# Post-norm and two stage-norm statistics taken token by partition on 128x4, and the first two units of the last up stage in one pass

## The chip, the cores and the metric

One core of a Trainium2 chip runs the whole program. The metric is device time in microseconds (us) of one execution; the median of three runs of the kernel before is 2634.64 us (2630.85 to 2634.64). TensorE's clock has two levels here, 2.4 GHz (granted clock 1.00 in the profile) and 1.2 GHz (0.50).

## What is computed

Two transformer blocks on 512 tokens of width 1024, in fp32. The change touches only the RMS norms:

```python
def rmsnorm(x, g):
    y = xf * lax.rsqrt(jnp.mean(xf * xf, axis=-1, keepdims=True) + RMS_EPS)
    return (y * g).astype(x.dtype)

# second block
f = swiglu(rmsnorm(x, ffn1_pre_g), ffn1_w_gate, ffn1_w_up, ffn1_w_down)
x = x + 0.5 * rmsnorm(f, ffn1_post_g)
y = hybrid_mixer(rmsnorm(x, mix_pre_g), ...)
x = x + rmsnorm(y, mix_post_g)
f = swiglu(rmsnorm(x, ffn2_pre_g), ffn2_w_gate, ffn2_w_up, ffn2_w_down)
x = x + 0.5 * rmsnorm(f, ffn2_post_g)
```

## The kernel before

Activations lie with the feature on the partition and the 512 tokens in the free dimension, as eight tiles of 128x512 (k = 0 to 7). Weights come in units of 128x1024 fp32 (eight 128x128 blocks, one output tile). Each unit is split: ScalarE makes w_hi (`high_part`, line 1075), GpSimd makes w_lo in two halves (line 336), and TensorE does 24 matmuls of 128x512 for it: per k one with h_hi and one with h_lo against w_hi (`mm_hi`), and then eight of h_hi against w_lo (`mm_lo`). These are fp32r. Units alternate between two weight buffers and between PSUM banks 0 and 1; SP loads the next raw weights when GpSimd has used the last. All matmuls go through one helper and are put down to line 363.

The norm is applied late: a unit is computed with the raw x times the gain, and the result is multiplied by 1/rms (`rst`) when VectorE takes it from PSUM (`take`, line 1525). A sum of squares over the features is a sum over partitions, so TensorE makes it, in plain fp32 (each such matmul is two records in the trace). The statistics are numbered by r. This change touches five of them:

- r = 3, 5, 7, the post norms after `down2`, `out2` and `down3`. VectorE sums the squares of the eight tiles into `acc` (line 2065), `stat_of_acc` (line 408) multiplies `acc` by a 128x128 block of ones, so that every partition of bank 2 holds the sums of all 512 tokens; ScalarE takes the square root from bank 2 to bank 3 (`stat_root`, line 1085), and VectorE the reciprocal in bank 3 (`rms_rstd`, line 1541). `post_scale` (line 2075) multiplies each tile by bank 3. Then per tile GpSimd adds it to x (line 348), ScalarE rounds h_hi and squares x (`residual_hi`, lines 1089 and 1093), and VectorE makes h_lo (`low_x`, line 1547). After r = 7 there is only the final addition and the store.
- r = 4 and 6, the norms ahead of the `mix` stage and of `up3`, the third up stage. They are made inside `first_unit`: as each tile k comes, TensorE does the two `mm_hi` of the stage's first unit, and one 128x512 matmul of the squares with ones into bank 2. After k = 7 it signals the sum, does the unit's eight `mm_lo`, and goes on to the second unit. VectorE's reciprocal goes to `rst` in SBUF and `ffn_dve` or the mix loop begins with `take`.

In `up3` ScalarE's order is: the root of r = 6, then (in `ffn_act`) a Silu of the first unit's taken result, and only then `high_part` of the stage's third unit.

Of the kernel before, what the change touches and what calls it, by code (L numbers as in the profile page):

```python
# [24 lines left out]
ACT = mybir.ActivationFunctionType  # L25
# [5 lines left out]
D = 1024  # L31
# [63 lines left out]
def build_program(nc, io):  # L95
# [3 lines left out]
    def sb(name, shape, dt=F32, scope=ctx):  # L99
        return scope.enter_context(nc.sbuf_tensor(name, shape, dt))  # L100
# [3 lines left out]
    def sem(name):  # L104
        if name not in sems:
            sems[name] = ctx.enter_context(nc.semaphore(name))
        return sems[name]

    with ctx:
# [12 lines left out]
        sel = sb("sel", [128, 8])  # L122
        rst = sb("rst", [128, T])
        eps, lnx_eps = sel[:, 3:4], sel[:, 4:5]
        psum = ctx.enter_context(nc.psum_tensor("psum", [128, 8, 512], F32))
# [143 lines left out]
        def tok(n):  # L269
            return slice(128 * n, 128 * n + 128)  # L270
# [90 lines left out]
        def _(pe):  # L361
# [48 lines left out]
            def first_unit(g, o, r, nset):  # L410
# [9 lines left out]
                for k in range(KD):  # L420
                    if k % 4 == 0:
                        open_low(g, k // 4)
                    last = mm_lo(psum[:, o.slot], g.slot, k, h_hi[:, k], k == KD - 1)
                last.then_inc(sem("unit_used"), 1)

            def spread_heads(bank, stat, c):
# [466 lines left out]
            def ffn_mm(f, hset, up, down, o, stat=None):  # L893
                if stat is None:
                    first_unit(Index(FIRST[up]), Index(o), 6, hset)
                else:
                    unit(Index(FIRST[up]), Index(o), h_hi, h_lo, ("h_ready", 8 * hset))
                    stat_of_acc(stat)
                unit(Index(FIRST[up] + 1), Index(o + 1), h_hi, h_lo)
                with pe.Fori(0, KF - 1) as i:  # L900
# [11 lines left out]
            ffn_mm(1, 3, "up2", "down2", 109, 1)  # L912
            stat_of_acc(2)
            first_unit(Index(FIRST["mix"]), Index(161), 4, 4)


# [143 lines left out]
            with pe.Fori(0, 4) as i:  # L1060
                for c in range(2):
                    unit(Index(FIRST["out2"] + c, i, 2), Index(254 + c, i, 2), y2_hi, y2_lo, ("y_ready", 8))
            stat_of_acc(3)
            ffn_mm(2, 6, "up3", "down3", 262)
            stat_of_acc(4)


        @block.scalar
        def _(act):
# [12 lines left out]
            def stat_root(r):  # L1082

                act.wait_ge(sem("stat_sum"), r + 1)
                act.activation(p3, p2, ACT.Sqrt, bias=eps, scale=1.0 / D).then_inc(sem("stat_root"), 1)

            def round_x(gains, k):
# [305 lines left out]
            down_tiles("down2", lambda last, i, c: square_f(109 + 2 * KF, last, i, c))  # L1393
            stat_root(3)

# [13 lines left out]
            residual_hi(0, "mix_pre")  # L1409
            stat_root(4)  # L1410
            with act.Fori(0, 2) as i:
# [96 lines left out]
            with act.Fori(0, 4) as i:  # L1508
                for c in range(2):
                    high_part(Index(FIRST["out2"] + 2 + c, i, 2))  # L1510
                    square_f(254, Index(FIRST["out2"] + c, i, 2), i, c)
            stat_root(5)
            residual_hi(1, "ffn2_pre")
            stat_root(6)
            ffn_act(2, "up3", 262)
            down_tiles("down3", lambda last, i, c: square_f(262 + 2 * KF, last, i, c), 1)
            stat_root(7)


        @block.vector  # L1520
        def _(dve):
# [15 lines left out]

            def rms_rstd(r, dst=rst[:]):

                dve.wait_ge(sem("stat_root"), r + 1)  # L1540
                dve.reciprocal(dst, p3).then_inc(sem("stat_rstd"), 1)  # L1541
                dve.wait_ge(sem("stat_rstd"), r + 1)

            def low_x(nset, gains, k):
# [510 lines left out]
            def f_tiles(stage, o, r, a, gains, factor, per_unit):  # L2055

                dve.memset(acc[:], 0.0).then_inc(sem("acc_done"), 1)
                with dve.Fori(0, 4) as i:
                    for c in range(2):
# [7 lines left out]
                                          ALU.mult, ALU.mult).then_inc(sem(f"freed{ob.slot}"), 1)  # L2067
                rms_rstd(r, p3)
                for c in range(2):
# [18 lines left out]
            residual_low(0, 4, "mix_pre")  # L2088
            rms_rstd(4)

# [161 lines left out]
            residual_low(1, 6, "ffn2_pre")  # L2252
            rms_rstd(6)
            ffn_dve(2, "up3", 262)
# [158 lines left out]
```

## Time and profile before

| | |
|---|---|
| median of three runs | 2634.64 us |
| profiled execution, its own time | 2633.49 us |
| its span, first to last instruction | 2631.4 us |
| mean granted TensorE clock | 0.966 |
| busy: PE, PEld (weight loads), DVE, ACT, POOL | 94%, 76%, 38%, 36%, 40% |
| chain that ended last | PE 87%, DVE 6%, ACT 4%, issue 2% |

The profile is read as follows. A row of the timeline or of the chain begins with its start in the span and its duration, in us; in the timeline rows of one kind in a row are merged, with their count. The end of a matmul is modelled, so the spacing of starts is what tells its price. A row of a stretch (window) holds per engine the busy us and the number of instructions, and then the granted clock (PEclk), the share of the DMA engines and GB/s.

### The profile page before, as it was taken

Reading aid. Unit: us, or ns where it says so; the run is one execution under the profiler, and the core shown is the slowest. Engines: PE = TensorE matmul, PEld = TensorE weight load, DVE = VectorE, ACT = ScalarE, POOL = GpSimd, SP = SyncE. Lnnn points to the kernel's source line nnn. Section 1 sums busy time; section 2 is a strip of 40 time slices with the busy share of each in tenths; the row PEclk is TensorE's granted clock in tenths of the full one; section 3 lists DMA queues with packets and bytes.
Section 4 is the critical chain, followed back from the end, with each engine's and each line's share of the span. In section 5 each row is a group of like instructions: output and inputs, shape, how many; then the busy total and the mean of one; then the engine's idle time right before and its main releaser. Section 6 shows DMA issues by size and latency. Waiting matters only on the chain.

```text
span 2631.4 us, 39196 instructions
## 1 busy us (share of the span) xinstructions
PE 2478.2 (94%) x14008; PEld 1986.8 (76%) x14008; DVE 991.8 (38%) x1684; ACT 954.8 (36%) x1283; POOL 1051.7 (40%) x756
## 2 busy tenths in 40 slices
PE   8989898889999999999998999998999998999997
PEld 6866777767788888788886677767777776788885
DVE  3244484554555522322214343334222244422213
ACT  3233342223566632444323122213443442444321
POOL 3211131014455555555555442342333344555554
PEclk9889999999999999999999999998999999999998
DMA  4111110013232233322332221121222222223332
GB/s 169 50 40 33 49 56 27 3 33 112 80 96 96 96 108 98 96 96 96 99 101 100 72 70 60 56 80 41 72 72 79 64 85 91 64 96 96 97 102 88
DMA packets 56744, 205.24 MB, mean 78 GB/s; under 512 B 6828, under 2 KB 7596, under 8 KB 56268
## 3 DMA queue, kind: packets, MB, share of 16 engines
q1 hardware_dynamic: 55152, 196.45, 23.0%
q10 hardware_dynamic: 1504, 7.49, 0.8%
q8 instruction: 71, 1.16, 0.2%
q14 instruction: 17, 0.14, 0.0%
HBM read 201.81 MB, written 2.10 MB: 77 GB/s over the span
## 4 chain that ended last, share of the span: by engine, by line
PE 87%; DVE 6%; ACT 4%; issue 2%; POOL 0%; DMA 0%; DVEq 0%; ACTq 0%; SPq 0%
PE psum L363 85%; DVE ml_qk L2181 1%; PE psum L541 1%; DVE tmp L1669 1%; ACT tmp L1166 1%; ACT w_hi L1075 0%; POOL x L348 0%; PE psum L975 0%; DVE psum L1541 0%; DVE zm L1739 0%; DVE inv L1840 0%; DVE rst L1541 0%; DVE psum L1530 0%; DVE tmp L2075 0%; ACT ml_qk L1454 0%
## 5 line engine op out<-in xcount | busy, mean ns | idle before, releaser
L336 POOL TENSOR_TENSOR w_lo<-raw,w_hi 128x512 fp32r<-128x512 f32 x732 | 1021.2, 1416 | 1549.2 <-ACT w_hi L1075 1549.2
L363 PE MATMUL psum<-h_hi,w_hi 128*128 128x512 f32 x2192 | 900.6, 411 | 57.5 <-DVE h_lo L1547 26.5
L363 PE MATMUL psum<-h_lo,w_hi 128*128 128x512 f32 x2192 | 871.7, 398 | 0.0
L1075 ACT ACTIVATE w_hi<-raw 128x1024 fp32r<-128x1024 f32 x366 | 386.0, 1055 | 834.4 <-PE psum L363 815.6
L363 PEld LDWEIGHTS psum<-h_hi,w_hi 128*128 128x128 f32 x2192 | 423.6, 193 | 191.8 <-issue 86.9
L363 PE MATMUL psum<-h_hi,w_lo 128*128 128x512 f32 x2192 | 550.6, 390 | 0.0
L363 PEld LDWEIGHTS psum<-h_lo,w_hi 128*128 128x128 f32 x2192 | 423.4, 193 | 90.7 <-issue 6.9
L363 PEld LDWEIGHTS psum<-h_hi,w_lo 128*128 128x128 f32 x2192 | 412.1, 188 | 87.5 <-issue 1.4
L1525 DVE TENSOR_TENSOR tmp<-psum,rst 128x512 f32<-128x512 f32 x108 | 74.7, 692 | 369.9 <-PE psum L363 369.5
L363 PE MATMUL psum<-hid_hi,w_hi 128*128 128x512 f32 x528 | 208.7, 395 | 0.0
L363 PE MATMUL psum<-hid_lo,w_hi 128*128 128x512 f32 x528 | 208.4, 395 | 0.0
L363 PE MATMUL psum<-hid_hi,w_lo 128*128 128x512 f32 x528 | 134.9, 395 | 0.0
L2065 DVE TENSOR_TENSOR acc<-acc,sq 128x512 f32<-128x512 f32 x24 | 30.8, 1283 | 242.9 <-ACT sq L1338 242.9
L363 PEld LDWEIGHTS psum<-hid_lo,w_hi 128*128 128x128 f32 x528 | 99.1, 188 | 24.1
L363 PEld LDWEIGHTS psum<-hid_hi,w_lo 128*128 128x128 f32 x528 | 99.1, 188 | 24.1
L363 PEld LDWEIGHTS psum<-hid_hi,w_hi 128*128 128x128 f32 x528 | 99.1, 188 | 24.1 <-DVE tmp L2038 0.2
L2049 DVE TENSOR_TENSOR hid_lo<-tmp,hid_hi 128x512 f32 x66 | 52.7, 798 | 60.7 <-ACT hid_hi L1387 60.7
L1383 ACT ACTIVATE tmp<-tmp 128x512 f32<-128x512 f32 x44 | 27.8, 632 | 115.4 <-DVE tmp L1525 115.4
L1387 ACT ACTIVATE hid_hi<-tmp 128x512 f32 x66 | 41.7, 632 | 70.5 <-DVE tmp L2047 70.5
L1166 ACT ACTIVATE tmp<-tmp,soft_nb,q_scale 128x128 f32<-128x128 f32 (+3 forms) x64 | 36.7, 643 | 83.8 <-DVE soft_nb L1677 83.8
L1530 DVE TENSOR_TENSOR psum<-psum,rst 128x512 f32<-128x512 f32 x60 | 41.6, 694 | 56.5 <-PE psum L363 56.3
L2034 DVE SCALAR_TENSOR_TENSOR tmp<-psum,par,tmp 128x511 f32<-128x511 f32 x44 | 33.0, 750 | 71.1 <-ACT tmp L1375 71.1
(383 smaller groups left out, 2552.1 us busy)
## 6 DMA issues: line engine op xcount, KB each, us to landing
raw<-in_w SPq DMA_DIRECT2D x366, 512.0 KB, 3.6
x<-in_x SPq DMA_DIRECT2D x4, 512.0 KB, 6.1
tmp<-in_cmp_w ACTq DMA_DIRECT2D x1, 2048.0 KB, 7.5
x<-in_x ACTq DMA_DIRECT2D x1, 2048.0 KB, 7.8
out_y<-x SPq DMA_DIRECT2D x8, 256.0 KB, 2.1
mask<-in_mask ACTq DMA_DIRECT2D x1, 1536.0 KB
masks<-in_masks ACTq DMA_DIRECT2D x1, 768.0 KB, 9.3
lora<-in_lora ACTq DMA_DIRECT2D x1, 512.0 KB, 4.2
```

The costliest lines, as they stand in the source:

```text
L336: pool.tensor_tensor(w_lo[:, g.slot, part], raw[:, g.slot, part], w_hi[:, g.slot, part].bitcast(F32), ALU.subtract).then_inc(sem("lo_ready ...
L363: return pe.matmul(out, lhsT, rhs, start=start, stop=stop)
L541: last = pe.transpose(psum[:, 6 + r, tok(m)], att_s[t % 2][2 * g + r][:, tok(m)], ident[:])
L1075: act.activation(w_hi[:, g.slot], raw[:, g.slot], ACT.Copy).then_inc(sem("hi_ready"), 1)
L1166: last = act.activation(p, p, ACT.Exp, bias=soft_nb[:, t % 2, g, r:r + 1], scale=q_scale[:, at:at + 1])
L1383: act.activation(tmp[:, 2], tmp[:, 4], ACT.Silu).then_inc(sem("silu_done"), 1)
L1387: act.activation(tile_of(hid_hi, i), tmp[:, 3], ACT.Copy).then_inc(sem("hid_rounded"), 1)
L1525: dve.tensor_tensor(dst, psum[:, o.slot], rst[:], ALU.mult).then_inc(sem(f"freed{o.slot}"), 1)
L1530: dve.tensor_tensor(psum[:, o.slot], psum[:, o.slot], rst[:], ALU.mult)\
L2034: dve.scalar_tensor_tensor(tmp[:, c, 1:], psum[:, ob.slot, 0:T - 1], col("ffn_conv", 2 * KF + c + 2 * i), tmp[:, c, 1:], ALU.mult, ALU.add ...
L2049: dve.tensor_tensor(tile_of(hid_lo, i), tmp[:, 3], tile_of(hid_hi, i).bitcast(F32), ALU.subtract)\
L2065: dve.tensor_tensor(acc[:], acc[:], sq[:, ob.slot], ALU.add).then_inc(sem("acc_done"), 1)
```

## The change

`stat_of_acc` gives way to `post_stat` at r = 3, 5 and 7, and `first_unit` to `first_units` at r = 4 (one unit) and r = 6 (two units). The matrix and the moving operand change places: for each of four blocks of 128 tokens, the squares are the stationary 128x128 operand and one column of ones is moved, so that the sum of a token stands on the token's partition, 128x4 in all. Root and reciprocal then work on 128x4 (`stat4`). `spread_rstd` brings the four columns back to all partitions: a column broadcast to 128x128 as the stationary operand, times the identity (128 columns), four times, into bank 3; TensorE waits for the reciprocal ahead of it, and VectorE waits for `stat_spread` behind it. For r = 4 and 6 VectorE copies bank 3 to `rst` and waits for the copy (`keep_rstd`). In `first_units` with two units, per k the order on TensorE is the first unit's `mm_hi`, the four statistic matmuls, the second unit's `mm_hi`; then the first unit's `mm_lo`, `spread_rstd`, the second unit's `mm_lo`.

```diff
+            def spread_rstd(r):
+                pe.wait_ge(sem("stat_rstd"), r + 1)
+                for b in range(TB):
+                    last = mm(p3[:, tok(b)], stat4[:, 1, b:b + 1].to_broadcast([128, 128]), ident[:])
+                last.then_inc(sem("stat_spread"), 1)
+            def post_stat(a, r):
+                pe.wait_ge(sem("acc_done"), 9 * a + 9)
+                for b in range(TB):
+                    last = mm(p2[:, b:b + 1], acc[:, tok(b)], sel[:, 2:3])
+                last.then_inc(sem("stat_sum"), 1)
+                spread_rstd(r)
+            def first_units(g, o, r, nset, count):
+                for n in range(count):
+                    open_unit(g + n)
+                    open_bank(o + n)
+                for k in range(KD):
+                    pe.wait_ge(sem("h_ready"), 8 * nset + k + 1)
+                    mm_hi(psum[:, o.slot], g.slot, k, h_hi[:, k], h_lo[:, k], k == 0)
+                    pe.wait_ge(sem("squared"), KD * r + k + 1)
+                    for b in range(TB):
+                        last = pe.matmul(p2[:, b:b + 1], tmp[:, k, tok(b)], sel[:, 2:3], start=k == 0 and b == 0,
+                                         stop=k == KD - 1, skip_group_check=True)
+                    if k == KD - 1:
+                        last.then_inc(sem("stat_sum"), 1)
+                    if count == 2:
+                        mm_hi(psum[:, (o + 1).slot], (g + 1).slot, k, h_hi[:, k], h_lo[:, k], k == 0)
+                for n in range(count):
+                    for k in range(KD):
+                        if k % 4 == 0:
+                            open_low(g + n, k // 4)
+                        last = mm_lo(psum[:, (o + n).slot], (g + n).slot, k, h_hi[:, k], k == KD - 1)
+                    last.then_inc(sem("unit_used"), 1)
+                    if n == 0:
+                        spread_rstd(r)
...
-                    first_unit(Index(FIRST[up]), Index(o), 6, hset)
+                    first_units(Index(FIRST[up]), Index(o), 6, hset, 2)
...
-            stat_of_acc(2)
-            first_unit(Index(FIRST["mix"]), Index(161), 4, 4)
+            post_stat(2, 3)
+            first_units(Index(FIRST["mix"]), Index(161), 4, 4, 1)
...
-            stat_of_acc(3)
+            post_stat(3, 5)
             ffn_mm(2, 6, "up3", "down3", 262)
-            stat_of_acc(4)
+            post_stat(4, 7)
...
+            def stat_root4(r):
+                act.wait_ge(sem("stat_sum"), r + 1)
+                act.activation(stat4[:, 0], p2[:, 0:TB], ACT.Sqrt, bias=eps, scale=1.0 / D).then_inc(sem("stat_root"), 1)
...
+            def rms_rstd4(r):
+                dve.wait_ge(sem("stat_root"), r + 1)
+                dve.reciprocal(stat4[:, 1], stat4[:, 0]).then_inc(sem("stat_rstd"), 1)
+                dve.wait_ge(sem("stat_spread"), r - 2)
+            def keep_rstd(n):
+                dve.tensor_copy(rst[:], p3).then_inc(sem("stat_kept"), 1)
+                dve.wait_ge(sem("stat_kept"), n)
```

The calls of `stat_root` and `rms_rstd` for r = 3 to 7 become `stat_root4` and `rms_rstd4`, with `keep_rstd` after r = 4 and 6. The statistics r = 0, 1 and 2 stay as they are.

## Rows read from the trace of the kernel before

**Rows 1.** Page, chain that ended last: share of the span by engine.

```profile
PE 87%; DVE 6%; ACT 4%; issue 2%; POOL 0%; DMA 0%; DVEq 0%; ACTq 0%; SPq 0%
```

**Rows 2.** Chain that ended last, 2225 to 2262 us: start, duration, what.

```profile
2230.41 1.14 PE psum L363 x2
...
2232.27 3.38 DVE psum L1541
...
2235.67 0.70 DVE tmp L2075
...
2239.63 22.54 PE psum L363 x72
```

**Rows 3.** Chain that ended last, 2608 to 2632 us.

```profile
2613.55 1.14 PE psum L363 x2
```

**Rows 4.** Small operations, each by its line: duration min/median/max in ns.

```profile
L1283 ACT ACTIVATE rs<-psum,sel x4: 260/264/268, 557.6 to 569.7; 128x8 f32<-128x8 f32 x4
...
L2210 DVE RECIPROCAL ml_small<-ml_small x4: 177/178/178, 1875.5 to 2096.8; 128x4 f32<-128x4 f32 x4
```

**Rows 5.** Timeline of TensorE, matmuls with few moving columns, and what follows.

```profile
65.61 12.46 PE L363 MATMUL psum<-blocks,tmp 64*64 64x31 f32 x256 [1.78 <-DVE blocks L1577]
...
84.96 4.20 PE L363 MATMUL psum<-sel,zm 128*128 128x2 f32 x32
89.02 0.77 PE L363 MATMUL psum<-h_hi,w_hi 128*128 128x512 f32 x1
```

**Rows 6.** The same, narrower stretches: its last six; 128x128 fp32 matmuls at 1597.

```profile
87.78 1.38 PE L363 MATMUL psum<-sel,zm 128*128 128x2 f32 x6
...
1597.47 1.52 PE L363 MATMUL psum<-att_pT,v_tm 128*128 128x128 f32 x12
```

**Rows 7.** Stretches around rows 5: busy us (x) of each engine, PEclk, DMA.

```profile
70.00:75.00 5.00, 5.00 (x99) 5.00 (x98) 0.00 (x0) 0.00 (x0) 0.00 (x0) 0.50 0.14 55
...
85.00:87.50 2.50, 2.50 (x25) 2.50 (x23) 0.69 (x1) 2.26 (x3) 1.14 (x1) 1.00 0.00 0
88.00:89.00 1.00, 1.00 (x6) 1.00 (x7) 0.00 (x0) 0.10 (x1) 0.85 (x1) 0.50 0.00 0
```

**Rows 8.** Stretches after the last unit ahead of r = 3, 5 and 7.

```profile
1422.50:1423.00 0.50, 0.00 (x0) 0.00 (x0) 0.50 (x1) 0.00 (x0) 0.00 (x0) 0.50 0.72 172
...
2231.50:2232.00 0.50, 0.04 (x1) 0.00 (x0) 0.00 (x0) 0.43 (x1) 0.00 (x0) 0.50 0.00 0
...
2612.00:2617.00 5.00, 1.18 (x3) 0.30 (x2) 2.94 (x3) 2.54 (x3) 0.00 (x0) 1.00 0.00 0
```

**Rows 9.** Timeline of TensorE through the first two units of up3 (r = 6).

```profile
2240.19 0.63 PE L363 MATMUL psum<-h_lo,w_hi 128*128 128x512 f32 x1
...
2242.75 0.63 PE L363 MATMUL psum<-h_lo,w_hi 128*128 128x512 f32 x1
...
2258.38 1.98 PE L363 MATMUL psum<-h_hi,w_lo 128*128 128x512 f32 x8
2260.20 0.39 PE L363 MATMUL psum<-h_hi,w_hi 128*128 128x512 f32 x1
```

**Rows 10.** Stretches of the loop of r = 4, and of that of r = 6.

```profile
1432.50:1433.00 0.50, 0.50 (x3) 0.36 (x3) 0.50 (x2) 0.50 (x2) 0.50 (x1) 0.81 0.00 0
...
2241.00:2245.00 4.00, 4.00 (x7) 1.80 (x6) 4.00 (x6) 3.11 (x6) 4.00 (x3) 0.50 0.00 0
2245.00:2246.00 1.00, 1.00 (x6) 0.68 (x4) 1.00 (x2) 0.55 (x2) 1.00 (x2) 0.97 0.00 0
```

**Rows 11.** Timeline of TensorE, first unit of mix (r = 4) and start of its second.

```profile
1429.54 0.77 PE L363 MATMUL psum<-h_hi,w_hi 128*128 128x512 f32 x1 [8.09 <-DVE h_lo L1547]
...
1444.16 0.39 PE L363 MATMUL psum<-h_hi,w_hi 128*128 128x512 f32 x1
```

**Rows 12.** Timelines of VectorE and ScalarE, from the reciprocal of r = 6 on.

```profile
2257.37 0.69 DVE L1525 TENSOR_TENSOR tmp<-psum,rst 128x512 f32<-128x512 f32 x1 [0.22 <-DVE rst L1541]
...
2258.63 1.04 ACT L1075 ACTIVATE w_hi<-raw 128x1024 fp32r<-128x1024 f32 x1
```

More of the change, by code:

```diff
@@ L123, in build_program @@
         rst = sb("rst", [128, T])
+        stat4 = sb("stat4", [128, 2, TB])
         eps, lnx_eps = sel[:, 3:4], sel[:, 4:5]
@@ L898, in ffn_mm @@
                     stat_of_acc(stat)
-                unit(Index(FIRST[up] + 1), Index(o + 1), h_hi, h_lo)
+                    unit(Index(FIRST[up] + 1), Index(o + 1), h_hi, h_lo)
                 with pe.Fori(0, KF - 1) as i:
@@ L1393, in _ @@
             down_tiles("down2", lambda last, i, c: square_f(109 + 2 * KF, last, i, c))
-            stat_root(3)
+            stat_root4(3)
             def residual_hi(m, gains):
@@ L1409, in _ @@
             residual_hi(0, "mix_pre")
-            stat_root(4)
+            stat_root4(4)
             with act.Fori(0, 2) as i:
@@ L1511, in _ @@
                     square_f(254, Index(FIRST["out2"] + c, i, 2), i, c)
-            stat_root(5)
+            stat_root4(5)
             residual_hi(1, "ffn2_pre")
-            stat_root(6)
+            stat_root4(6)
             ffn_act(2, "up3", 262)
             down_tiles("down3", lambda last, i, c: square_f(262 + 2 * KF, last, i, c), 1)
-            stat_root(7)
+            stat_root4(7)
         @block.vector
@@ L1536, in low_h, with rms_rstd @@
                     .then_inc(sem("h_ready"), 1)
-            def rms_rstd(r, dst=rst[:]):
+            def rms_rstd(r):
                 dve.wait_ge(sem("stat_root"), r + 1)
-                dve.reciprocal(dst, p3).then_inc(sem("stat_rstd"), 1)
+                dve.reciprocal(rst[:], p3).then_inc(sem("stat_rstd"), 1)
                 dve.wait_ge(sem("stat_rstd"), r + 1)
+            def rms_rstd4(r):
[5 more added lines that the diff above has]
+                dve.wait_ge(sem("stat_kept"), n)
             def low_x(nset, gains, k):
@@ L2067, in f_tiles @@
                                           ALU.mult, ALU.mult).then_inc(sem(f"freed{ob.slot}"), 1)
-                rms_rstd(r, p3)
+                rms_rstd4(r)
                 for c in range(2):
@@ L2088, in _ @@
             residual_low(0, 4, "mix_pre")
-            rms_rstd(4)
+            rms_rstd4(4)
+            keep_rstd(1)
             with dve.Fori(0, 2) as i:
@@ L2252, in _ @@
             residual_low(1, 6, "ffn2_pre")
-            rms_rstd(6)
+            rms_rstd4(6)
+            keep_rstd(2)
             ffn_dve(2, "up3", 262)
```

## The prediction

> **What bounds the kernel now.** I read the chain that ended last first: TensorE holds 87% of it [rows 1], so what an edit is worth is what it does to TensorE's own time, or to the few places where TensorE stands still. Then I read the chain through r = 5 and 6. From the sum of `acc` to the first `post_scale` everything is serial: statistic matmul at 2230.41, root, reciprocal at 2232.27 for 3.38 us, and the product at 2235.67, 5.26 us in all; TensorE starts the stage's k loop at 2239.63 and from there to 2262 the chain is TensorE alone [rows 2]. So the reader is to see two regimes: a serial stretch, where the reciprocal is most of the price, and a k loop in which TensorE is the bound and never waits. Third I looked at the granted clock, since TensorE stands idle before each such loop: it had fallen to 0.50 by 1422.5 and by 2231.5 [rows 8], and came back inside the loops, at about 1432.7 and 2245.0 [rows 10]. There is no slack of TensorE in the loop of r = 6 for the second unit to fill: it works off what the slow start left behind.
>
> **Prices.** A 128x512 fp32r matmul costs 0.23 us at 1.00 (eight from 2258.38 to 2260.20) and 0.43 at 0.50 (2240.19 to the statistic that follows; the whole k step of the kernel before, two of them and an fp32 one of 1.7 us, is 2242.75 - 2240.19 = 2.56) [rows 9]. For the new statistic matmul (fp32, 128x128 stationary, one column) the nearest row is the head statistics, 128x128 by two columns, two records each. Of its 32 records 26 start from 84.96 to 87.78, 0.11 us each, at clock 1.00; the last six take 87.78 to 89.02, 0.21 each, at 0.50 [rows 5, 6, 7]. Eight records are therefore 0.9 us per k at full clock and 1.7 at half, the same as the 512-column product that they replace (1.7 at half). The change of sides saves TensorE nothing: the time goes to loading the stationary operand. One column against two changes no load; I take the same and no gain. `spread_rstd` is eight records with 128 columns. Its nearest row is twelve such in 1.52 us [rows 6], less about 0.28 for the last one's end and over 11 spacings, 0.11 each: 0.9 us at full clock, 1.7 at half.
>
> The Trainium skill, "TensorE: Matmul & The Clock Gate", section LDWEIGHTS (loading the stationary operand), prices a load by its columns alone, 107 ns for 128, with no word of the granted clock. The trace agrees at 1.00 and not at 0.50, where a record took 0.21. By the page a k step of r = 4 at half clock would be 0.86 + 0.86 = 1.7 us in place of 2.56, and both loops together would give some 13 us less than my sum; the measured spacing decides.
>
> **Part 1, the serial stretches of r = 3, 5, 7.** Before: 5.26 us. After: statistic 1.2 (first load 0.15, seven spacings of 0.11, end 0.25; before 1.14), root on 128x4 0.26 and reciprocal on 128x4 0.18 [rows 4] with 0.03 of hop each, then hop, load, eight records and end: 1.35 at full clock, 2.2 at half. Sum 3.05 or 3.9; the gain is 2.2 or 1.35. With the 512-column product gone the clock has nothing to keep it up: it had fallen by 1422.5 and 2231.5 even with it [rows 8], about when the spread will run, so for r = 3 and 5 I take 1.4 each. In the tail it was still 1.00 until 2617 [rows 8], counted from the same product at 2613.55 [rows 3]; the spread ends near 2616.5, so I take 2.2. Together -5.0 us (-4.0 to -6.6). Next in line after each is `post_scale`, as before; the DMAs that ScalarE issues behind the root of r = 3 shift with it and are not waited for until mix's second unit.
>
> **Part 2, the clock in the k loops.** This decides the sum. What the trace shows: a burst of 128x2 matmuls at 84.96, following dense work and with TensorE busy without a gap, had the clock at 1.00 until 87.5 and at 0.50 from 88 on [rows 5, 7]. 256 records of 64x31, 12.5 us of a fully busy TensorE, ran at 0.50 (70 to 75 is one stretch of it) [rows 5, 7]. The clock came back at 1432.7 and 2245.0 after 3.1 and 5.4 us of unbroken 512-column work from 1429.54 and 2239.63 [rows 2, 10, 11]. In the new loops the loads of the small matmuls take two thirds of each k at r = 4 (1.7 of 2.56) and half at r = 6 (1.7 of 3.42), in turn with 512-column ones. No row of the trace shows such a mixture. I take it that the small matmuls do not bring the clock up, as they did not hold it, and that the loops, which begin at 0.50, stay there to their ends. The other end, the clock as before, is a rival.
>
> The same page of the Trainium skill says in Part 1 and in its last table that the clock follows how busy the engine is: keep it busy without gaps and it runs at full level. By that rule both loops, in which TensorE never idles, would come back to 2.4 GHz as before; that is rival A, 2632 us. The trace agrees for 512-column work and disagrees for the two small bursts.
>
> **Part 3, r = 4 (one unit).** Before: from 1429.54 to the second unit's first matmul at 1444.16 is 14.6 us [rows 11], of which eight `mm_lo` are 1.8, so the loop is 12.8. After: 8 x 2.56 = 20.5, +7.7. The tiles come every 1.7 us, faster than that, so nothing else bounds it. Behind the loop the eight `mm_lo` and the spread are unbroken again; the clock returns 3.1 to 5.4 us later, which costs half of that, +2.2 (1.5 to 2.8). The spread itself +0.9; TensorE's wait for the reciprocal costs nothing, since root and reciprocal (0.5) lie beside `mm_lo` (1.8 at least). The reciprocal of 3.36 us that goes was hidden under the second unit, and so is the copy to `rst`. Sum +10.8 (10.0 to 11.6).
>
> **Part 4, r = 6 (two units).** Before: 2239.63 to the third unit's first matmul at 2260.20, 20.6 us [rows 9]. After: a k step is four 0.43 and 1.7, 3.42 us; eight are 27.4. Then `mm_lo` 1.8, spread 0.9 and the clock's return 2.2: 4.9. Now the third unit does not follow behind the second's `mm_lo` (1.8), because its w_hi comes late: the spread's end 0.2, the copy to `rst` 0.7 (as the `take` from PSUM, 0.69) and its wait 0.2, then `take` to ScalarE's w_hi finished, 2257.37 to 2259.67, and 0.1 to TensorE [rows 12]: 3.5 us. This was hidden by 5.4 us of second unit; the interleaving takes the cover away and costs 1.7 of wait. Sum 27.4 + 4.9 + 3.5 = 35.8, +15.2 (14.3 to 16.0). What lies behind (w_lo, raw loads, Silu) keeps its distance to the third unit.
>
> **The sum** is made against the profiled execution, 2633.49 us, 1.15 below the median: 2633.5 - 5.0 + 10.8 + 15.2 = 2654.5 us, with its own range 2651 to 2658.
>
> **Rivals.** A, the clock comes back in the loops as it did before. Then at r = 4, 3.1 to 5.4 us at half (1.2 to 2.1 steps) and the rest at 1.36 per k: 12.4 to 13.5, with the spread about +1.0; at r = 6 (0.9 to 1.6 steps, the rest at 1.81), 16.0 to 17.1 + 2.7 + 3.5, about +2.2. Total 2633.5 - 5.0 + 3.2 = 2631.7. For it: nothing in the trace shows the mixture. Against: both bursts. Chance 0.08. B, only the loop with two units, half of it 512-column work, brings it back: -5.0 + 10.8 + 2.2, 2641.5. Chance 0.08. C, the faster side: the idle stretch ahead of the loops (8.1 us before, some 5 after, with the spread in it) becomes too short for the clock to fall, and it holds. The posts gain 2.2 each, r = 4 is paced by the tiles (12.3 + 0.9 + 1.8, +0.4), r = 6 is 8 x 1.81 + 2.7 + 3.5 = 20.7, +0.1: 2627.4. It decides from a clock of 1.00 at the first k; against it, the clock fell before with dense work closer behind. Chance 0.03. D, the wait of 1.7 us at r = 6, next to the small matmuls, drops the clock once more: +3, 2657.5. Chance 0.05. That the change does not do what it says would be that `stat4` spreads the same sums at another price; it is in A to D. The forecast keeps 0.76.
>
> **Range and chances.** A measurement of this kernel can tell about 0.2%, 5.3 us, from no change. The range takes in the forecast, B and D, 2641 to 2659, and leaves out A and C. Slower by over 0.2% (from 2639.9): forecast, B and D, 0.89; within: A, 0.08; faster: C, 0.03.
>
> **What the profile after would show.** Post stretch: 3.9 us from the statistic to `post_scale` at r = 3 and 5, near 3.0 in the tail. r = 4: PEclk 0.50 through the loop, `mm_hi` starts 2.56 apart per k, loop 20.5 us. r = 6: 0.50 through 27 us, then a wait of TensorE of 1.7 us for w_hi at the third unit. If PEclk is 1.00 in the later k steps, with 1.36 and 1.81 us per k, the forecast is wrong and A holds; if it is so at r = 6 only, B. If a statistic record is not 0.21 at half clock, the prices were.

## The result, and the profile after

| | before | after |
|---|---|---|
| median | 2632.74 us (4 runs, 2626.88 to 2634.64) | 2649.90 us (4 runs, 2648.10 to 2654.06) |
| profiled execution | 2633.49 us | 2648.10 us |
| its span | 2631.4 us | 2646.1 us |
| mean granted clock | 0.966 | 0.961 |

The ratio of after to before is 1.0071, with a 95% interval of 1.005 to 1.0093: the change makes the kernel slower, by 17.2 us in the medians and 14.6 in the profiled executions. The forecast was 2654.5 in a range of 2641 to 2659, slower with 0.89; the forecast's own range was 2651 to 2658, and the measured median lies 1.1 us below that.

The page of after gives each engine's busy time and, of the chain that ended last, the shares by engine and by line:

```profile
PE 2503.3 (95%) x14162; PEld 2023.1 (76%) x14162; DVE 978.0 (37%) x1686; ACT 952.6 (36%) x1283; POOL 1051.1 (40%) x756
...
PE 88%; DVE 5%; ACT 3%; issue 3%; DMA 0%; DVEq 0%; ACTq 0%; POOL 0%; SPq 0%
PE psum L364 85%; PE psum L452 1%; DVE ml_qk L2239 1%; PE psum L582 1%; DVE tmp L1726 1%; ACT tmp L1212 1%; ACT w_hi L1116 1%; PE psum L1016 0%; DVE zm L1796 0%; DVE inv L1897 0%; DVE rst L1587 0%; DVE psum L1576 0%; DVE tmp L2132 0%; ACT ml_qk L1500 0%; ACT zm L1352 0%
```

VectorE's share of the chain fell from 6% to 5% and ScalarE's from 4% to 3%, and TensorE's rose from 87% to 88% [rows 1]. The new entry, line 452, is the statistic matmuls of `first_units`. So the chain moved in the direction that the sum had: less on VectorE and ScalarE, which hold the serial stretches, more on TensorE.

**The serial stretches.** The chain of after at r = 3, then in the tail (start, duration, what):

```profile
1417.39 1.07 PE psum L364 x8
...
1418.48 0.27 ACT stat L1131
...
1418.78 0.19 DVE stat L1593
...
1419.01 2.09 PE psum L364 x8
...
1421.13 0.70 DVE tmp L2132
...
2629.60 1.27 PE psum L364 x8
...
2631.43 2.09 PE psum L364 x8
...
2633.54 1.30 DVE tmp L2132 x2
```

From the statistic to the first `post_scale` it is now 3.73 us (1421.13 - 1417.39), where it was 5.26 [rows 2]. Root and reciprocal together last 0.46. Most of what the shorter root and reciprocal save is spent on the spread: 2.09 us for eight records, here and at r = 5 and 7 alike, its price at half clock.

**The loop of r = 4.** TensorE's timeline in after:

```profile
1425.09 0.76 PE L364 MATMUL psum<-h_hi,w_hi 128*128 128x512 f32 x1 [4.00 <-DVE h_lo L1604]
...
1426.07 1.70 PE L452 MATMUL psum<-sel,tmp 128*128 128x1 f32 x8
1427.63 0.77 PE L364 MATMUL psum<-h_hi,w_hi 128*128 128x512 f32 x1
...
1445.55 3.76 PE L364 MATMUL psum<-h_hi,w_lo 128*128 128x512 f32 x8
1449.11 1.14 PE L364 MATMUL psum<-ident,stat 128*128 128x128 f32 x8
1450.01 0.48 PE L364 MATMUL psum<-h_hi,w_hi 128*128 128x512 f32 x1
```

The idle time ahead of it halved, 4.00 us for 8.09 [rows 11]: here the shorter post is to be seen. Then a k step takes 2.54 us (1427.63 less 1425.09), and so do all eight (1445.55 - 1425.09 = 20.5), and the second unit starts 24.9 us after the loop's start, where it was 14.6 [rows 11].

**The loop of r = 6**, the same view:

```profile
2240.66 0.77 PE L364 MATMUL psum<-h_hi,w_hi 128*128 128x512 f32 x1 [4.00 <-DVE h_lo L1604]
...
2243.21 0.77 PE L364 MATMUL psum<-h_hi,w_hi 128*128 128x512 f32 x1
...
2268.10 3.61 PE L364 MATMUL psum<-h_hi,w_lo 128*128 128x512 f32 x8
2271.51 1.24 PE L364 MATMUL psum<-ident,stat 128*128 128x128 f32 x8
2272.51 2.09 PE L364 MATMUL psum<-h_hi,w_lo 128*128 128x512 f32 x8
2276.14 0.49 PE L364 MATMUL psum<-h_hi,w_hi 128*128 128x512 f32 x1 [1.54 <-ACT w_hi L1116]
```

27.4 us for eight k steps, then a wait of 1.54 us for the third unit's w_hi; from the loop's start to the third unit it is 35.5 us and was 20.6 [rows 2, 9].

**The clock.** Stretches of after: busy us (records) of PE, PEld, DVE, ACT and POOL, then the granted clock, the DMA share and GB/s.

```profile
1426.00:1445.00 19.00, 19.00 (x77) 17.57 (x75) 9.57 (x11) 7.45 (x12) 8.51 (x6) 0.50 0.02 7
...
1449.00:1450.00 1.00, 1.00 (x9) 0.90 (x9) 0.00 (x0) 0.65 (x1) 0.00 (x0) 0.85 0.00 0
...
2241.00:2267.00 26.00, 26.00 (x94) 23.10 (x93) 10.16 (x12) 7.69 (x13) 9.09 (x6) 0.50 0.00 0
...
2272.00:2273.00 1.00, 1.00 (x9) 0.96 (x9) 0.21 (x1) 0.00 (x0) 0.00 (x0) 1.00 0.00 0
2629.00:2630.00 1.00, 0.40 (x4) 0.40 (x4) 1.00 (x2) 1.00 (x1) 0.00 (x0) 1.00 0.00 0
2630.00:2634.00 4.00, 2.93 (x14) 2.55 (x14) 0.85 (x3) 0.30 (x2) 0.00 (x0) 0.54 0.00 0
```

This is nearly the whole loss, as e4 below shows. In both loops the profile has TensorE busy for every us of the stretch and the granted clock is 0.50 (1.2 GHz) from end to end, where before it was back at 1432.7 and 2245.0, a few us into the loop [rows 10]. It comes back only behind them, in the unbroken `mm_lo` and the spread. The Trainium skill, "TensorE: Matmul & The Clock Gate", Part 1, lets the clock follow how busy the engine is. If busy means what the profile counts as busy, the trace disagrees: 26.00 busy us of 26.00 ran at 0.50. It agrees with what the prediction took from its two bursts. The last two rows show the tail: 1.00 as the statistic starts, 0.50 under the spread.

**Where the time went.** To compare traces without the shift that they gather, I number ScalarE's 366 w_hi operations from 0 and measure between starts: 193 to 196 holds r = 3 and r = 4, and 365 to the end of the span holds the tail. The stretch of r = 5 and 6 begins with operation 298 and ends with TensorE's first matmul of `up3`'s fourth unit; from there on the units of all kernels here keep the same distance. (The w_hi of the third unit is no good end for it: e7, e8 and e10 move just this operation, and e3 shifts it against the matmuls that use it.) Together I call them the touched places; the rest of the span computes the same in every kernel here. Against the profiled execution of before, in us:

| after, by its trace | forecast | measured |
|---|---|---|
| post and loop, r = 3 and 4 | -1.4 + 10.8 = +9.4 | +8.9 |
| post and loop, r = 5 and 6 | -1.4 + 15.2 = +13.8 | +13.5 |
| tail, r = 7 | -2.2 | -1.3 |
| touched places together | +21.0 | +21.1 |
| all the rest | 0 | -6.4 |
| span | +21.0 | +14.7 |

Of the -6.4, 2.9 us had been gained before r = 3, where the two programs do the same, so this part is not the change's work, and 2.4 came in the mix stage behind r = 4, where the code is also the same but the start is shifted. The first goes with the granted clock: ahead of operation 193 it was 0.50 for 92 us in before and for 85 in after. In the mix stage (operations 196 to 220) it was so for 3.4 us and for none, which at twice the speed is worth 1.7 us at most, so not all of the 2.4. A piece of it, six products of 512 columns in the mix stage, in the timeline of before,

```profile
1680.70 3.00 PE L363 MATMUL psum<-qk_st 128*128 128x512 f32 x6 [0.69 <-ACT v_tm L1418]
```

and the same six in that of after:

```profile
1683.88 2.17 PE L364 MATMUL psum<-qk_st 128*128 128x512 f32 x6 [0.69 <-ACT v_tm L1464]
```

The first ran at 0.50 (1681 to 1684 in before), the second at 1.00 (1684 to 1687 in after). Which of such short stretches fall to half clock differs from one execution to the next: the runs of before shown with the experiments below lie between 2624.4 and 2641.5 us, at a mean granted clock of 0.969 and 0.962.

### The profile page after: what moved, and what is told of

It reads as the page before. It is cut to its first block, busy times and chain, and to the rows that moved or that the text cites. A ratio compares the mean times of both kernels' runs of the same rounds, so it can differ in the third digit from the quotient of the medians.

```text
span 2646.1 us, 39506 instructions
## 1 busy us (share of the span) xinstructions
PE 2503.3 (95%) x14162; PEld 2023.1 (76%) x14162; DVE 978.0 (37%) x1686; ACT 952.6 (36%) x1283; POOL 1051.1 (40%) x756
## 4 chain that ended last, share of the span: by engine, by line
PE 88%; DVE 5%; ACT 3%; issue 3%; DMA 0%; DVEq 0%; ACTq 0%; POOL 0%; SPq 0%
PE psum L364 85%; PE psum L452 1%; DVE ml_qk L2239 1%; PE psum L582 1%; DVE tmp L1726 1%; ACT tmp L1212 1%; ACT w_hi L1116 1%; PE psum L1016 0%; DVE zm L1796 0%; DVE inv L1897 0%; DVE rst L1587 0%; DVE psum L1576 0%; DVE tmp L2132 0%; ACT ml_qk L1500 0%; ACT zm L1352 0%
```

## The experiments

The question was what holds the clock down in the two loops, and which part of the change is worth keeping. Every experiment is read by the same three intervals. The first two columns of this table are medians and their ratio to the runs of before on the same chip (its medians there were 2635.14, 2635.11 and 2634.81 us, for e1, e2, e4, e5, for e3, e6, e7, e8, and for e9, e10); the others come from the profiled execution of each kernel, against that of before. After and the three groups were measured apart from each other. The profiled execution need not be a typical one: that of e8 (2614.59) is its fastest of seven, that of e7 (2634.39) its slowest of ten.

| kernel | us (runs) | ratio, 95% interval | r = 3, 4 | r = 5, 6 | tail | touched | rest |
|---|---|---|---|---|---|---|---|
| after | 2649.90 (4) | 1.0071, 1.005 to 1.0093 | +8.9 | +13.5 | -1.3 | +21.1 | -6.4 |
| e1_posts_only | 2629.23 (12) | 0.9976, 0.9965 to 0.9988 | -1.4 | -2.0 | -2.3 | -5.8 | -1.1 |
| e2_norms_only | 2662.35 (1) | | +12.5 | +15.8 | 0.0 | +28.3 | +0.6 |
| e3_one_unit_r6 | 2650.62 (1) | | +10.0 | +9.9 | -2.4 | +17.4 | -0.2 |
| e4_wide_columns | 2627.95 (10) | 0.9975, 0.9963 to 0.9986 | +0.4 | +2.2 | -1.2 | +1.4 | -4.5 |
| e5_warm | 2631.43 (1) | | +7.0 | -1.0 | -1.5 | +4.5 | -7.7 |
| e6_dense_two_units | 2628.87 (1) | | -1.5 | +0.8 | -2.4 | -3.2 | -1.5 |
| e7_order | 2629.71 (10) | 0.9978, 0.9965 to 0.9991 | +0.4 | +0.6 | -2.0 | -1.1 | +2.1 |
| e8_filled | 2626.06 (7) | 0.9962, 0.9947 to 0.9977 | -1.3 | -2.6 | -2.4 | -6.4 | -12.5 |
| e9_posts_filled | 2626.50 (6) | 0.9968, 0.9956 to 0.998 | -2.3 | -2.8 | -2.4 | -7.5 | +0.7 |
| e10_filled_again | 2622.44 (6) | 0.995, 0.9936 to 0.9963 | -0.9 | -3.5 | -2.5 | -6.9 | -4.7 |

The last column is the lesson of the table: the rest goes from -12.5 to +2.1 us though nothing in it was edited, more than most of the effects in question. So single executions are compared by the touched places, and totals only by medians with an interval. Even so the two do not always agree. The medians of e1 and e9, whose norms of r = 4 and 6 are the old ones, lie 0.2 and 0.8 us further below before than their touched places say; those of after, e4, e7, e8 and e10, with the new norms, lie 4.0, 8.6, 4.3, 2.6 and 5.5 us lower than theirs. No run shows why.

### e1 and e2: the change in two halves

e1 keeps the new posts and takes the old norms of r = 4 and 6:

```diff
-            first_units(Index(FIRST["mix"]), Index(161), 4, 4, 1)
+            first_unit(Index(FIRST["mix"]), Index(161), 4, 4)
...
-                    first_units(Index(FIRST[up]), Index(o), 6, hset, 2)
+                    first_unit(Index(FIRST[up]), Index(o), 6, hset)
+                    unit(Index(FIRST[up] + 1), Index(o + 1), h_hi, h_lo)
...
```

> The 128x4 statistics of r = 3, 5 and 7 stay, r = 4 and 6 are as in the kernel before. If the small statistics in the k loops are the whole loss (clock theory), this is faster than before by 1.35 us per post at half clock and 2.2 at full, 4 to 6.6 us in all, 0.15 to 0.25%, and both k loops are as long as before (12.8 us, and 20.6 us to the third unit of up3). If the posts themselves take part in the loss (spread and extra hops dearer than reasoned), it is not faster.

e2 is the other half, new norms with the old posts:

```diff
-            post_stat(2, 3)
+            stat_of_acc(2)
...
-            post_stat(3, 5)
+            stat_of_acc(3)
...
-            post_stat(4, 7)
+            stat_of_acc(4)
...
```

> The other half alone: r = 4 and 6 as in the changed kernel, the posts as before. Clock theory: both loops at granted clock 0.50 throughout, 20.5 and 27.4 us; the two stages cost 10.8 + 15.2 = 26 us against before, so some 2656 to 2660 us, about 4 to 5 us more than the changed kernel. If the idle stretch ahead (again 8 us) mattered for the length of the slow part, the loops would differ from those of the changed kernel; they should not.

e1's posts took 3.84, 3.73 and 2.94 us in place of three times 5.26, and its loops 12.40 and 12.39 us (before 12.39 and 12.87). Its median is 5.9 us below that of before, and the whole interval lies below 1. e2's posts took 6.21, 6.13 and 5.26, its loops 20.47 and 27.45, the same as in after (20.47 and 27.44), at the same clock:

```profile
1433.00:1452.00 19.00, 19.00 (x77) 17.62 (x75) 9.52 (x11) 7.45 (x12) 8.46 (x6) 0.50 0.00 1
2254.00:2281.00 27.00, 27.00 (x96) 23.96 (x96) 10.26 (x13) 8.39 (x15) 9.02 (x6) 0.50 0.00 1
```

So the posts are a gain and the loops more than the whole loss. e2's two longer posts are the same 512-column product at half clock, 2.09 us in its chain for 1.14, as the clock had fallen a little earlier. Its one execution came to 2662.35 us, above the 2656 to 2660 that were expected.

### e4: the same instructions with 128 moving columns

Only the moving operand of the statistic differs: the matrix of ones in place of its one column. Number of matmuls, stationary operands and their loads stay; the root reads every 128th column of the bank at r = 4 and 6.

```diff
-                        last = pe.matmul(p2[:, b:b + 1], tmp[:, k, tok(b)], sel[:, 2:3], start=k == 0 and b == 0,
+                        last = pe.matmul(p2[:, tok(b)], tmp[:, k, tok(b)], ones, start=k == 0 and b == 0,
...
```

> The changed kernel with one thing different: each statistic matmul of the two k loops moves 128 columns of ones in place of one column (the four sums are then read with a step of 128). As many matmuls, the same stationary loads; at full clock 128 fp32 columns cost 0.11 us per record, what the load costs anyway. Clock theory: the clock comes back inside both loops 3 to 5.5 us after their start, k steps 1.36 and 1.81 us after that, loops 12.4 to 13.5 us (r = 4) and 16 to 17 (r = 6), 16 to 19 us less than the changed kernel, about 2631. Rival, that the loads or the number of instructions are what is slow: no gain, 2650.

TensorE's timeline in e4, from the start of the loop of r = 4:

```profile
1426.82 0.77 PE L364 MATMUL psum<-h_hi,w_hi 128*128 128x512 f32 x1 [4.00 <-DVE h_lo L1605]
...
1427.81 1.91 PE L452 MATMUL psum<-sel,tmp 128*128 128x128 f32 x8
1429.37 0.78 PE L364 MATMUL psum<-h_hi,w_hi 128*128 128x512 f32 x1
...
1432.91 0.48 PE L364 MATMUL psum<-h_hi,w_hi 128*128 128x512 f32 x1
...
1433.45 1.05 PE L452 MATMUL psum<-sel,tmp 128*128 128x128 f32 x8
1434.26 0.48 PE L364 MATMUL psum<-h_hi,w_hi 128*128 128x512 f32 x1
```

and its stretches at r = 6:

```profile
2235.00:2240.00 5.00, 5.00 (x19) 4.43 (x19) 5.00 (x7) 3.67 (x7) 5.00 (x4) 0.50 0.00 0
2240.00:2251.00 11.00, 11.00 (x74) 9.94 (x74) 5.19 (x6) 4.08 (x7) 4.13 (x3) 1.00 0.00 0
```

The first k step takes 2.55 us, as in after; from 1432.91 on it is 1.35. The loops are 12.86 and 17.16 us instead of 20.47 and 27.44, together 17.9 us less, though each statistic matmul moves 128 times the columns. At half clock eight records cost 1.56 us (1427.81 to 1429.37) with 128 columns as with one (1426.07 to 1427.63 in after), so the columns are free there. This settles the cause in the part that was disputed: it is not the number of matmuls nor the loads of the stationary operand that holds the clock at 0.50 but that the statistic moves one column. By its touched places e4 would be 1.4 us above before; its median is 7.2 below. In the profiled execution 4.5 us of the difference lie in the rest, and of them some 2 in the mix stage (operations 196 to 220), which is shorter by 2.4, 2.0, 2.4, 2.0 and 2.4 us in after, e4, e5, e7 and e8, by 0.5, 0.3, 0.3 and 0.7 in e2, e3, e10 and e1, and longer by 1.2 and 2.1 in e6 and e9. Where before was at 0.50 for 3.4 us of this stage, after, e5 and e8 were so for none of it, and e2, e3, e6, e9 and e10 for 10.2; but e4 and e7 were so for 3.4 as well, so the clock alone does not account for it, and the cause stays open.

### e5: the same loops, entered at full clock

After, with 16 dense 128x512 products (their results are unused) in TensorE's idle time ahead of both loops:

```diff
+            def warm(g, count, half=1):
+                open_unit(g)
+                open_low(g, half)
+                for n in range(count):
+                    mm(p4, w_hi[:, g.slot, 0:128], w_lo[:, g.slot, 0:512])
...
             def first_units(g, o, r, nset, count):
+                warm(g, 16)
```

> The changed kernel with 16 matmuls of 128x512 (results unused) ahead of each of the two k loops, in the idle stretch; at half clock they take 6.9 us, more than the idle stretch of 4, so each loop starts up to 3 us later. Clock theory: the loops start at 1.00. That of r = 4, with a statistic share of two thirds, falls to 0.50 again within some us; that of r = 6, half 512-column work at 1.81 us per k, may stay at 1.00: 14.5 us in place of 27.4. Then about 10 us less than the changed kernel. If it is the small matmuls' own cost, the loops stay 20.5 and 27.4 us and it is 5 us slower.

Three stretches of e5 (the loop of r = 4 starts at 1424.93, that of r = 6 at 2237.49 and ends at 2252.09):

```profile
1425.00:1429.00 4.00, 3.82 (x28) 3.42 (x26) 4.00 (x6) 2.79 (x5) 4.00 (x3) 1.00 0.14 46
...
1430.00:1442.00 12.00, 12.00 (x48) 11.04 (x48) 5.22 (x6) 4.10 (x7) 4.15 (x3) 0.50 0.00 1
2237.50:2252.00 14.50, 14.50 (x97) 13.14 (x97) 10.51 (x12) 8.26 (x15) 9.45 (x6) 1.00 0.00 1
```

Both loops began at 1.00. That of r = 4, where the one-column matmuls are two thirds, fell to 0.50 some 4 us in, with TensorE busy for 3.82 us of 4, and stayed there: 17.60 us. (In e8 below the same loop with 128 columns was entered at 1.00 too, and held it to its end: 12.79 us.) That of r = 6, where they are half, held 1.00 to its end: 14.60 us, against 27.44 for the same instructions in after. So the mixture of r = 6 keeps the level that it finds, low or high, and that of r = 4 does not keep the high one. It is one execution; at 2631.43 us it is 18 us below the median of after, where about 10 were expected.

### e3 and e6: what the pass of two units does

e3 is after with one unit in the loop of r = 6 and the second behind it:

```diff
-                    first_units(Index(FIRST[up]), Index(o), 6, hset, 2)
+                    first_units(Index(FIRST[up]), Index(o), 6, hset, 1)
+                    unit(Index(FIRST[up] + 1), Index(o + 1), h_hi, h_lo)
```

> The changed kernel, but r = 6 with one unit in its k loop (as r = 4) and the second unit behind it. Clock theory: granted clock 0.50 through the loop, 8 x 2.56 = 20.5 us in place of 27.4, then 1.8 + 0.9 + 2.2 + 5.5: the third unit of up3 starts 30.9 us after the loop's start, 4 to 5 us earlier than in the changed kernel (35.5). If it is the interleaving that does the harm and not the small matmuls, it is as fast as before here (20.6 + 0.9).

e6 has both units in the pass but the old statistic in it, a product with 512 moving columns, and the root and reciprocal on 128x512 that go with it; r = 4 is as in the kernel before:

```diff
-                    for b in range(TB):
-                        last = pe.matmul(p2[:, b:b + 1], tmp[:, k, tok(b)], sel[:, 2:3], start=k == 0 and b == 0,
-                                         stop=k == KD - 1, skip_group_check=True)
+                    last = mm(p2, ones, tmp[:, k], k == 0, k == KD - 1)
...
```

> Posts on 128x4, r = 4 and 6 with the 512-column products of the kernel before, but at r = 6 the two units in one pass. Clock theory: the clock comes back within the loop; loop of r = 6 about 16 to 17 us (3.42 at half, 1.8 at full clock per k), no spread. The third unit then waits for root 0.7, reciprocal 3.4 and 2.6 us more on VectorE and ScalarE, 6.7 behind the loop against 3.7 of mm_lo: it starts 23 us after the loop's start, 2 to 3 us later than before. If interleaving keeps the clock down, 27 us and more.

In e3 the second unit runs behind the slow loop, at full clock: its first matmul, and the third unit's.

```profile
2274.38 0.48 PE L364 MATMUL psum<-h_hi,w_hi 128*128 128x512 f32 x1
...
2279.93 0.39 PE L364 MATMUL psum<-h_hi,w_hi 128*128 128x512 f32 x1
```

The loop took 20.47 us at 0.50, as that of r = 4 does. From its start at 2248.78 it is 31.15 us to the third unit, 4.3 less than in after (35.48): that is what the second unit's products cost for lying in a loop at half clock and taking the cover from w_hi. In e6 the clock came back, the loop took 16.30 us, and then

```profile
2257.87 0.49 PE L364 MATMUL psum<-h_hi,w_hi 128*128 128x512 f32 x1 [2.64 <-ACT w_hi L1112]
```

TensorE waited 2.64 us, since root and reciprocal of 128x512 stand ahead of the third unit's w_hi with no second unit to hide them. From loop start to third unit e6 needs 22.74, before 20.57. With the old statistic the pass of two units costs 2.2 us and brings nothing: in before, TensorE was the bound there and the second unit was work to be done either way.

### e7: the third unit's w_hi ahead of the Silu

e4 with ScalarE's order changed at the one place where TensorE waits:

```diff
+                        if f == 2:
+                            high_part(Index(FIRST[up] + 2, i, 2))
                         act.wait_ge(sem(f"freed{gb.slot}"), gb.half() + 1)
                         act.activation(tmp[:, 2], tmp[:, 4], ACT.Silu).then_inc(sem("silu_done"), 1)
-                        for c in range(2):
+                        for c in range(f - 1, 2):
```

> The kernel with 128 moving columns in the loops (e4_wide_columns) and one change of order on ScalarE: in up3, w_hi of the third unit ahead of the first Silu. If the wait of TensorE for w_hi is what the interleaving costs at r = 6 (1.5 us in e4), the third unit starts 1.5 us earlier, 21.9 us after the loop's start in place of 23.4, and what follows keeps that. Total 1.5 us below e4_wide_columns. If the next weights or the Silu are late in turn, less.

The third unit's first matmul in e4,

```profile
2258.17 0.49 PE L364 MATMUL psum<-h_hi,w_hi 128*128 128x512 f32 x1 [1.54 <-ACT w_hi L1116]
```

and in e7:

```profile
2263.09 0.50 PE L364 MATMUL psum<-h_hi,w_hi 128*128 128x512 f32 x1
```

The wait is gone, and loop start to third unit went from 23.45 to 21.74 us (21.9 expected). In the totals this is not to be seen: 2629.71 against 2627.95 in e4, the wrong way, measured apart, with intervals that overlap nearly whole. The expected 1.5 us are less than this kernel's own spread can show.

### e8, e9, e10: filling the idle time

e8 is e7 with dense products of unused result (`warm`, as in e5) in TensorE's idle time around every post:

```diff
+            warm(Index(FIRST["mix"]), 10)
             post_stat(2, 3)
+            warm(Index(FIRST["mix"]), 14)
...
+            warm(Index(FIRST["up3"]), 10)
             post_stat(3, 5)
+            warm(Index(FIRST["up3"]), 14)
...
+            warm(Index(UNITS - 1), 5)
             post_stat(4, 7)
```

> e7_order with 128x512 matmuls (results unused) in TensorE's idle stretches: 10 ahead of the statistic of r = 3 and 5, 5 ahead of that of r = 7, 14 between spread and k loop at r = 4 and 6. Clock theory: granted clock 1.00 from the last unit through the post norm and the loop. Posts 3.0 us each in place of 3.9 to 4.4 in e4; loop of r = 4 paced by the tiles, 12.3 us; loop of r = 6 14.5 us. Against e7_order 1 us per post and some 2.4 us at r = 6, about 5 us in all; against before 0.3 to 0.45%. If the fillers come in the way of the statistic or the first tile, less than that.

e8 is faster than before, its interval is 0.9947 to 0.9977. Its loops took 12.79 and 14.63 us, both at 1.00 throughout, and its posts 2.81, 3.73 and 2.81: at r = 5 the filler did not hold the clock through the spread, which took 2.1 again. What in it does the work? e9 is e1, the old norms and a single unit at r = 6, with the same `warm` lines; e10 is the kernel of e8 again, beside it.

> The kernel of e1 (posts on 128x4, the statistics of r = 4 and 6 as before the change: 512-column products, root and reciprocal on 128x512, one unit at r = 6) with e8's filler matmuls at the same places: 10 dense 128x512 products ahead of the statistics of r = 3 and 5, 14 behind, 5 ahead of r = 7; their results are unused. Question: how much of e8's 9 us below the kernel before comes from the filler and the posts, and how much from the columns and the pass of two units. Theory (the filler and the posts are nearly all of it): posts 2.8 each if the filler holds 1.00 through them (3.7 where it doesn't), the loop of r = 4 is paced by the tiles at 12.3 (first unit to second 14.2, before 14.63), r = 6 about 12.3 + 1.8 + 5.4 = 19.5 to its third unit (before 20.57). Against e1 (posts 3.84, 3.73, 2.94, loops 14.64 and 20.07) that is about -3 us: 2626, ratio 0.9965, not distinguishable from e8. Rival (the columns and the two units are what e8 gains by): at least 3 us above e8 run beside it, 2629 or more, ratio 0.998 or more. Second rival: with the 512-column product in the loops they are no quicker than in e1, since they are paced by the tiles; then the filler brings 1 to 2 us in the posts only, 2627.5.

> The kernel of e8 once more, beside e9 on the same chip, since two medians taken in different calls lie as far apart as the effect in question. Theory: 2626 again (0.9962 of the kernel before, 0.995 to 0.998), posts 2.8, 2.8 to 3.7, 2.8, the two loops 12.8 and 14.6 us long, to the next unit 15.5 and 19.2. Rival: e8's ratio was the luck of which short stretches ran at 0.50; then it comes out at 0.998 to 0.999, as e1, e4 and e7.

e9's posts were 2.82, 2.82 and 2.90 us, e10's 3.24, 2.81 and 2.81. The stretch of post and loop at r = 5 and 6, first in e9,

```profile
2228.00:2248.00 20.00, 17.27 (x62) 9.89 (x62) 15.23 (x19) 10.94 (x18) 14.66 (x10) 1.00 0.08 27
```

then in e10:

```profile
2224.00:2247.00 23.00, 20.79 (x130) 18.23 (x130) 15.44 (x20) 11.78 (x20) 14.69 (x10) 1.00 0.07 24
```

and the spread in e10's chain:

```profile
2226.50 1.17 PE psum L364 x8
```

The clock held 1.00 through both, and the spread took 1.17 us for the 2.09 of after. Of the touched places e9 has -7.5, e8 -6.4 and e10 -6.9: the new norms add nothing there to what posts and filler give. In e10 they cost 0.7 us at r = 4 (second unit 15.34 us after the loop's start, 14.65 in e9) and bring 0.8 at r = 6 (third unit 19.27 after it, 20.09 in e9); its post of r = 3 took 3.24 where 2.8 was expected. e9 stayed with the second rival for its loops, which are no quicker than in e1 (12.41 for 12.40, paced by the tiles), and gained 2.0 us on e1 in the posts, the upper end of that rival's 1 to 2. Its total, 2626.50, is what the theory said; but e10 beside it came to 2622.44, 4.1 lower, a distance that the first rival asked for, though not its 2629. The two intervals (0.9956 to 0.998 and 0.9936 to 0.9963) overlap by a hair. Since the touched places explain none of the 4.1, I leave open whether the new norms with wide columns help elsewhere. The kernel of e8 and e10, the best here, beats before by 9.1 us in the one measurement and 12.4 in the other, and after, measured apart from them, by some 24 to 27.

## Why the prediction was right

**Prices.** Right. A k step at half clock was put at 2.56 and 3.42 us, and was 2.56 (20.47 / 8) and 3.43 (27.44 / 8). A statistic record was put at 0.21 us at half clock, and what a k step has left beside its 512-column products at 0.43 is that; between starts eight take 1.56, 0.20 each. The Trainium skill's rule in the LDWEIGHTS section of "TensorE: Matmul & The Clock Gate", a load priced by its columns alone, would have made the k step of r = 4 1.7 us; the runs decide against it at half clock. At full clock eight start within 0.81 us (e4, 1433.45 to 1434.26), 0.10 each, near the 107 ns of the Trainium skill.

**Part 1, the posts.** Forecast 3.9, 3.9 and 3.05 us; measured 3.73, 3.73 and 3.94, so gains of 1.5, 1.5 and 1.3 for 1.4, 1.4 and 2.2. The step that failed is the tail's: the prediction carried the clock of before, 1.00 until 2617 [rows 8], over to a kernel whose product there had shrunk, and let the spread run at it. In after the stretch from 2630 is at 0.54, and the spread took its half-clock 2.09. The price of that term was right at the other level: in e1, e3, e6, e8, e9 and e10, whose tails kept the clock longer, that post took 2.8 to 2.9. The error is 0.9 us. The smaller product is not the reason, as it is in these tails too; the same code took 3.28, 3.73 and 4.10 us in e7, e5 and e4, by when the clock fell. The posts of r = 3 and 5 vary likewise: where the statistic itself ran at half clock (e3, e4, e7, and r = 3 of e5) they took 4.45 to 4.55, a case that the prediction, with 1.2 us for the statistic at either level, did not have. The old post at such a clock took 6.21 (e2), so that the new one gains 1.7 there too.

**Part 2, the clock.** Right, and it carried the sum. That matmuls with few columns do not bring the clock back was read from two bursts elsewhere in the trace [rows 5, 7] and held in a mixture that no row of before showed; the step from the bursts to the mixture was a guess that came true. What the prediction had only as a guess, e4 shows: the columns moved are the difference. e5 adds what it lacked: entered at 1.00, the loop of r = 6 stayed there in the one execution taken. That is rival C's condition (1.00 at the first k), made by filler products, with C's result at r = 6, 14.60 for its 14.5, and not at r = 4, where C said 12.3 and 17.60 came. C's condition isn't met in after, where the idle time ahead of the loops is still 4.00 us. One reading has to be put right: of the burst of 256 records that starts at 65.61, the first 1.8 us ran at 1.00, and only the rest at 0.50, so the clock fell under it as it did under the other.

**Part 3, r = 4.** Forecast +10.8, by the timeline +10.3 (24.92 for 14.62). The loop's 20.5 us are exact, but the loop of before is 12.39 and not 12.8, as its eight `mm_lo` took 2.24 and not 1.8 (they start at 1441.92, the second unit at 1444.16 [rows 11]):

```profile
1441.92 2.40 PE L363 MATMUL psum<-h_hi,w_lo 128*128 128x512 f32 x8
```

The loop cost +8.1, not +7.7. What stands behind it was put at 4.9 us in all and took 4.5, and cost +2.2, not +3.1.

**Part 4, r = 6.** Forecast +15.2, measured +14.9. From the loop's end to the third unit 8.4 us were forecast and 8.0 measured; the wait for w_hi, put at 1.7, was 1.54, with the chain behind the spread as it was worked out (copy to `rst`, `take`, w_hi).

**The sum.** +21.0 was forecast for the touched places and they cost +21.1; that it is so near is in part luck, as errors of up to 0.9 us in its terms cancel. The prediction missed the profiled time by 6.4 us and the median by 4.6, because the rest of the span ran 6.4 us shorter than in the profiled execution of before. It took one execution's course of the clock outside the change for granted. With the rest between -12.5 and +2.1 us in eleven profiled executions, it should have been a term of the range. As it was, both times lie below the forecast's own 2651, and it was the room left for rival B, whose mechanism did not occur, that held them.

**Rivals.** A (2631.7) and B (2641.5) fell with 0.50 through both loops. A's numbers for a loop whose clock returns, 12.4 to 13.5 and 16.0 to 17.1 us, are what e4 shows, 12.86 and 17.16. D, the wait of 1.54 us dropping the clock once more, did not happen: 1.00 from 2272, and the third unit's matmuls 0.23 apart.

## What to carry to other kernels

An fp32 matmul with a new stationary operand cost TensorE as much here with one moving column as with 128, and with one it can cost the clock of the whole loop that it stands in: if such matmuls must stand among dense ones, move 128 columns and ignore the surplus. Read the granted clock at the entry of a loop as well as inside it, for the same loop took 27.4 or 14.6 us by the level that it was entered with, and idle time ahead of it can be filled with products that nobody needs. Turning a statistic round pays on the serial path, where the 128x512 reciprocal stood in the way (here 0.7 to 2.4 us a place against the 5.26 of before, by the clock that statistic and spread meet), and not under a unit that hid it.

## What the runs showed of the hardware

- A fully busy TensorE stayed at 0.50 for 26 us, and fell from 1.00 to 0.50 some 4 us into a loop without a gap worth the name (e5, r = 4: 3.82 of 4.00 us busy, then 12.00 of 12.00 at 0.50). Both loops hold one-column matmuls among those of 512 columns.
- One mixture of matmuls ran at the level that it was entered with: r = 6 of after at 0.50 in 27.44 us, and the same loop in e5 at 1.00 in 14.60 (one execution).
- fp32 matmuls with a new 128x128 stationary operand each take 0.20 us a record at half clock whether they move 1 or 128 columns (1.56 us for eight, after and e4); at full clock they are 0.10 for both (0.81 us for eight, e5 and e4).
- The parts of the program that nobody touched varied by 14.6 us between profiled executions, with short stretches at 0.50 that came and went. Before operation 193 all kernels here have the same code, and it took from 9.1 us less (e8) to 4.6 us more (e7) than in before, with 79 and 106 us at 0.50 for 92. A difference of 5 us between two single executions of this kernel says nothing.
